# Dense gates of a PEER layer: one-hot tables built token by token with per-partition scalars

## The reference, cut to what matters

```python
s1 = jnp.einsum('thd,hnd->thn', q[:, :, 0], P['peer_k1'][layer])
s2 = jnp.einsum('thd,hnd->thn', q[:, :, 1], P['peer_k2'][layer])
v1, i1 = lax.top_k(s1, PEER_TOPK)
v2, i2 = lax.top_k(s2, PEER_TOPK)
...
best, pos = lax.top_k(cand, PEER_TOPK)
idx = jnp.take_along_axis(cidx, pos, axis=-1)
gates = jax.nn.softmax(best, axis=-1)
...
act = jax.nn.gelu(jnp.einsum('td,ted->te', xb, u_tab[ib])) * gb
return jnp.einsum('te,ted->td', act, v_tab[ib])
```

## Time and profile before

| what | value |
|---|---|
| median of 3 runs | 5684.04 us (5681.76 to 5685.91) |
| the profiled execution, its own time | 5684.63 us |
| span of the profiled execution | 5682.8 us |
| busy VectorE / GpSimd / TensorE matmul | 3780.8 / 2301.7 / 4550.2 us |
| dense gates of layer 0, first to last GpSimd instruction | 2028.56 us, for 188.85 us |
| dense gates of layer 1, the same | 4308.20 us, for 188.84 us |

### The profile page before, as it was taken

How to read it: one execution, slowest core, us unless ns; L and a number is a source line. 1 busy time by engine, 2 the same in 40 slices (tenths; PEclk the granted TensorE clock), 3 DMA queues, 4 the chain that set the end, 5 groups by cost and what they waited for, 6 DMA issues and landing times. The chain is left out here.

```text
span 5682.8 us, 72188 instructions
## 1 busy us (share of the span) xinstructions
PE 4550.2 (80%) x24898; PEld 3778.9 (66%) x24898; DVE 3780.8 (67%) x6636; ACT 1540.3 (27%) x2465; POOL 2301.7 (41%) x1748
## 2 busy tenths in 40 slices
PE   3668769778778754999999948887884499999995
PEld 0347748658566744999999944433574499999994
DVE  1143452543524986999999973241498689999997
ACT  0122222322211133333333321110123333333332
POOL 0021312412311486566666640000148656666664
PEclk8779779788789877999999979878997799999997
DMA  9110000000011025999999951101102499999996
GB/s 388 48 47 15 1 14 2 14 14 1 3 64 67 1 59 161 389 396 407 405 396 406 404 188 56 56 19 63 67 1 59 142 387 399 407 404 398 406 403 226
DMA packets 382991, 1049.09 MB, mean 185 GB/s; under 512 B 36647, under 2 KB 168999, under 8 KB 376616
## 3 DMA queue, kind: packets, MB, share of 16 engines
q0 software_dynamic: 147456, 536.94, 24.1%
q1 hardware_dynamic: 235368, 509.88, 24.0%
HBM read 990.62 MB, written 56.07 MB: 184 GB/s over the span
## 5 line engine op out<-in xcount | busy, mean ns | idle before, releaser
L733 PE MATMUL bank<-h_parts,u_parts 128*128 128x384 f32 x6144 | 1117.6, 336 | 98.8 <-DVE u_parts L808 98.8
L733 PEld LDWEIGHTS bank<-h_parts,u_parts 128*128 128x128 f32 x6144 | 1083.9, 189 | 118.6 <-issue 99.1
L743 PE MATMUL bank<-v_parts,gg_parts 128*128 128x512 f32 x4608 | 1095.7, 391 | 0.0
L705 POOL DMA_INDIRECT u_rows<-in_u_rows,rows_idx x512 | 696.4, 1360 | 770.8 <-DVE dots L812 665.1
L743 PEld LDWEIGHTS bank<-v_parts,gg_parts 128*128 128x128 f32 x4608 | 861.2, 188 | 170.6
L818 DVE SCALAR_TENSOR_TENSOR rows_y<-v_rows,row_scale,rows_y 128x1024 f32<-128x1024 f32 x512 | 660.4, 1291 | 27.8 <-DVE row_scale L823 14.1
L711 POOL DMA_INDIRECT v_rows<-in_peer_v,rows_idx x512 | 607.9, 1187 | 168.8 <-issue 153.7
L812 DVE CUSTOM_DVE_ANT_0 u_rows<-u_rows,rows_h 128x1024 f32<-128x1024 f32 x512 | 621.9, 1215 | 0.0
L604 DVE TENSOR_TENSOR hot<-selT,iota 128x1024 f32<-128x1024 f32 x192 | 376.7, 2038 | 34.5 <-PEq L618 34.5
L302 POOL TENSOR_TENSOR x<-x,gb 128x1024 f32<-128x1024 f32 x20 | 47.9, 2395 | 830.3 <-ACT x L295 830.3
L613 POOL TENSOR_TENSOR hot<-hot,selT 128x512 f32<-128x512 f32 x192 | 377.7, 2004 | 11.2 <-DVE hot L604 11.2
(11 more groups left out here) (300 smaller groups left out, 6454.4 us busy)
## 6 DMA issues: line engine op xcount, KB each, us to landing
hT<-in_peer_u SPq DMA_DIRECT2D x260, 512.0 KB
v_in<-in_peer_v SPq DMA_DIRECT2D x256, 512.0 KB
w_modt<-in_w_mod SPq DMA_DIRECT2D x24, 2048.0 KB, 24.7
gates<-gates_sb SPq DMA_DIRECT2D x6, 8192.0 KB, 30.4
g_in<-gates SPq DMA_DIRECT2D x256, 192.0 KB
wq<-in_peer_wq SPq DMA_DIRECT2D x32, 512.0 KB, 11.5
w_hy<-in_hy_w_in SPq DMA_DIRECT2D x9, 1536.0 KB, 6.5
w_rkv<-in_w_rkv SPq DMA_DIRECT2D x6, 1536.0 KB, 6.4
```

The costliest lines, as they stand in the source:

```text
L705: pool.indirect_dma_start(ug[n % GR][:, :], None, m.i["u_rows"], bass.IndirectOffsetOnAxis(ap=R.idx[:, n % 2, n // 2:n // 2 + 1], axis=0)) ...
L733: mm = pe.matmul(m.bank[j % 2][:, 0:TD], us[:, j % 2, a, k, :], hs[:, b, k, :], start=(k == 0 and i == 0), stop=(k == KD - 1 and i == 2))
L743: mm = pe.matmul(yb[t][c][:, :], gs[:, j, a, t * P:(t + 1) * P], vs[:, j % 2, b, c * BANK:(c + 1) * BANK], start=(first and i == 0), stop= ...
```

## The change

Both tables are now built one token at a time, on two engines side by side. VectorE makes the first keys' table with a tensor_scalar: `m.iota` is compared with the token's first key and multiplied by its gate, both of which are read as one value per partition from `selT`. GpSimd makes the second keys' table with a tensor_scalar that compares `m.iota` with the second key, again one value per partition. Neither waits for the other. Both wait for TensorE to release the slot, and TensorE waits for both. The loops of VectorE and GpSimd are written out. TensorE's loop gets one more wait; ScalarE and SyncE are unchanged.

```diff
-        table = [P, 2, QT, NKEY]
         with nc.Block() as block:
             @block.vector
             def _(dve):
-                with dve.Fori(0, BLOCKS * GROUPS // TBLS) as r:
-                    for u in range(TBLS):
-                        k = TBLS * r + u
+                for k in range(BLOCKS * GROUPS):
+                    u = k % TBLS
+                    if k >= TBLS:
                         dve.wait_ge(s["pg_mm"], k + 1)
-                        dve.tensor_tensor(hot[:, u], selT[:, 0:2, bass.ds(k * QT, QT)].unsqueeze(3).broadcast_to(table),
-                                          m.iota[:, :].unsqueeze(1).unsqueeze(1).broadcast_to(table), ALU.is_equal).then_inc(s["pg_hot"], 1)
+                    for q in range(QT):
+                        t = k * QT + q
+                        ins = dve.tensor_scalar(hot[:, u, 0, q, :], m.iota[:, :], selT[:, 0, t:t + 1], selT[:, 2, t:t + 1], ALU.is_equal, ALU.mult)
+                    ins.then_inc(s["pg_gated"], 1)
 
             @block.gpsimd
             def _(pool):
-                with pool.Fori(0, BLOCKS * GROUPS // TBLS) as r:
-                    for u in range(TBLS):
-                        k = TBLS * r + u
-                        pool.wait_ge(s["pg_hot"], k + 1)
-                        pool.tensor_tensor(hot[:, u, 0], hot[:, u, 0], selT[:, 2, bass.ds(k * QT, QT)].unsqueeze(2).broadcast_to([P, QT, NKEY]),
-                                           ALU.mult).then_inc(s["pg_gated"], 1)
+                for k in range(BLOCKS * GROUPS):
+                    u = k % TBLS
+                    if k >= TBLS:
+                        pool.wait_ge(s["pg_mm"], k + 1)
+                    for q in range(QT):
+                        t = k * QT + q
+                        ins = pool.tensor_scalar(hot[:, u, 1, q, :], m.iota[:, :], selT[:, 1, t:t + 1], None, ALU.is_equal)
+                    ins.then_inc(s["pg_hot"], 1)
@@ tensor @@
                         pe.wait_ge(s["pg_gated"], k + 1)
+                        pe.wait_ge(s["pg_hot"], k + 1)
                         pe.wait_ge(s["pg_sb"], k + 1)
```

## The result

The changed kernel takes 5751.81 us (median of 4 runs, 5750.43 to 5759.29) against 5684.98 us of the kernel before beside it: a ratio of 1.0124, 95% interval 1.0112 to 1.0136, or 67 us slower. The forecast was 5811 us in a range of 5700 to 5960.

What follows compares the result with a forecast made beforehand. VectorE and GpSimd taking turns were taken to bound the dense gates: 384 tokens at 0.66 us give 253.4 us per layer against 190.28, +126 for two layers on 5684.63, hence 5811 us, range 5700 to 5960.

Steps and rivals of the forecast that it cites:

- rival 3: Dense gates: no interference, GpSimd alone sets 0.579 us per token, +64 us, 5749 us; chance 0.12 for 5700 to 5765.
- GpSimd's instruction, 0.579 us from line 1130: Dense gates: GpSimd's new comparison costs 0.579 us per token, like line 1130's 128 elements with a scalar per partition.
- The scalar per partition makes it dear: GpSimd's tensor_scalar: the per-partition scalar makes line 1130's 608 ns, as line 520 with constants takes 298 ns.
- VectorE's turn adds to GpSimd's, 0.66 us per token: Dense gates: the engines take turns, 0.646 us by streaming or 0.681 by measured overlap; 0.66 us per token taken.
- lock for the whole instruction: Shared ports held for each whole instruction: 0.955 us per token, +353 us, 6038 us; chance 0.08 for 5960 and above.
- VectorE's median well above its minimum: Sign in the changed profile: VectorE's median well above its minimum of about 0.35 us, mostly as long as GpSimd's turn.
- The cheap form as a rival: GpSimd's comparison takes 0.298 us as line 520: 0.365 us per token, -100 us, 5584 us; chance 0.10.
- TensorE, ScalarE and unrolling hidden: Dense gates: matmuls 1.16, weight loads 1.78, ScalarE 1.05 us stay under 2.64 us per group; written-out code priced at nothing.
- weight loads of 1.78 us would surface with a group at 1.5 us: Dense gates, TensorE: with a group at 1.5 us, its weight loads at 1.78 us would no longer be hidden.
- One-input operations on GpSimd at roughly line-rate: Skill's statement on GpSimd's one-input operations, cited for the faster rival; the prediction said rows agree for constants only.

Runs made afterwards that it cites:

- run 1: Changed kernel with VectorE making only the first four groups' tables, so GpSimd works alone: 5749.46 us.
- run 2: Changed kernel with GpSimd comparing with a constant instead of the token's second key: 5719.86 us.
- Run 5: Changed kernel with VectorE making the first keys' table by two tensor_tensor of 512 elements per group (compare, then multiply by gates): 5829.43 us.
- run 3: Changed kernel with GpSimd's comparison replaced by mult and add with two constants on the same buffers: 5577.80 us.
- run 7: Kernel before with VectorE's and GpSimd's loops written out and the first four groups not waiting for TensorE: 5686.09 us, ratio 1.0000.
- run 9: Changed kernel with GpSimd making two of a group's four second-key tokens, VectorE the rest by one tensor_tensor: 5576.24 us; with one token on GpSimd, 5603.23 us.
- run 8: Changed kernel without GpSimd's block and TensorE's wait for it; VectorE makes the second table with one more tensor_tensor: 5618.62 us, ratio to before 0.9888.

## Why the prediction came out as it did

The direction, the bound and the place were right, and 5751.8 us lies in the range. It lies outside the forecast's own band of 5765 to 5860, which had a chance of 0.50. It is not the forecast of 5811 but the number of rival 3 (5749, no interference), to which the prediction gave 0.12; the range held because it was made wide enough to take that rival in.

- *GpSimd's instruction, 0.579 us from line 1130.* Right: 0.577 alone (run 1).
- *The scalar per partition makes it dear.* Half right. It makes arithmetic dear (298 to 608 ns), but a comparison is dear anyway (527, run 2), so the reason was wrong for this instruction though the price was right.
- *VectorE's turn adds to GpSimd's, 0.66 us per token.* This is the mis-sized term. It was forecast at about 0.08 us and measured at 0.008. The difference between 0.66 and 0.585 us, over 768 tokens of both layers, is 58 us, and 5811 - 58 = 5753 is what was measured. The step behind it was to carry over as "a GpSimd instruction holds the path from start to end". Run 5 shows that the comparison of 128 elements leaves the path free for about 0.3 us. The instructions of 640 elements in the earlier trace rows did keep VectorE waiting to their end; why they differ, no run shows. The Trainium skill's lock for the whole instruction ("SBUF — State Buffer", "Who interferes with whom") does not agree with the changed kernel: to the letter it gave 0.955 us per token and 6038 us, where 0.585 was measured.
- *VectorE's median well above its minimum.* Wrong: 346 against 331 ns.
- *The cheap form as a rival.* It is not what the change does. Its 5584 us is 6 us from run 3 (5577.8) by luck: VectorE's turn costs GpSimd nothing there, and the 0.346 us per token is GpSimd's own mean pace, with an instruction of 0.298 us.
- *TensorE, ScalarE and unrolling hidden.* Right: weight loads of 1.78 us fit into 2.34, and run 7 shows nothing for the loops. That weight loads of 1.78 us would surface with a group at 1.5 us did not come true: in run 9 a group takes 1.42 us, and the last section says what became of TensorE's clock.
- *One-input operations on GpSimd at roughly line-rate* (the Trainium skill, "GPSIMD Engine Reference", section 4.1): of four forms the rows and runs show only one, at 298 ns, that comes near VectorE's 226 ns; the others take 527 to 608.

What stays open is the exact rule of the hand-over. The amounts that GpSimd pays per group for VectorE streams of about 0.27, 0.40, 0.50 and 1.07 us are 0.03, 0.11, 0.25 and 0.41 us. A free part of 0.3 us per GpSimd instruction explains the last, but would hide streams of 0.13 us wholly, and would hide part of the 0.27 us stream of run 9, which cost 0.26. Who reaches the path first has a part in it; so may the fact that four VectorE instructions come in a burst, two to a GpSimd instruction. No run separates these.

## What to carry to other kernels

Before moving an operation to GpSimd, look for a row of that very form: operation, constant or scalar per partition, length. Here four forms of one instruction on 128 elements lie between 298 and 608 ns, and the change put 384 of a dear one on the path in each layer. When two engines slow each other, ask which one could do all of it alone: VectorE alone was 1.1% faster than before, and with half of the second table left to GpSimd, so that both engines take about as long, 1.9%.

## What the hardware showed that was not expected

TensorE's granted clock went together with how closely its work came. The windows over the dense gates of layer 0 (us, then busy us of PE, PEld, DVE, ACT and POOL, granted clock, DMA share, GB/s), of the run with long VectorE instructions (run 5), of the changed kernel and of VectorE alone (run 8):

```profile
2027.00:2287.00 260.00, 194.18 (x760) 169.21 (x760) 149.06 (x191) 99.27 (x94) 260.00 (x384) 0.50 0.23 65
```

```profile
2027.00:2247.00 220.00, 157.88 (x744) 137.62 (x744) 117.62 (x384) 97.22 (x93) 219.82 (x376) 0.69 0.27 76
```

```profile
2027.00:2180.00 153.00, 108.96 (x741) 92.02 (x742) 152.17 (x469) 97.15 (x92) 0.00 (x0) 0.97 0.39 110
```

With a group every 2.72 us the clock is 0.50, the lower level of 1.2 GHz throughout, and every group's weight loads take 1.78 us. With a group every 2.34 us the mean is 0.69, a mix of 2.4 and 1.2 GHz, and about half of the groups' weight loads take 1.78 us. With a group every 1.62 us it is 0.97, and nearly all take 0.97 us. I had feared 2.05 us per group from TensorE in runs 8 and 9. It did not come: where the tables came faster, the clock was higher too. The runs show that the two go together; they do not separate what the clock answers to.
